# A gather of expert rows through six buffers in place of eight

## The reference, cut to what matters

```python
def peer_ffn(h, wq, sub_keys, u, v):          # 256 tokens, two tiles of 128
    q = (xt @ wq)...                          # 8 heads
    s = einsum(q, sub_keys)                   # 2 x 128 key scores a head
    ...                                       # top 16 of the 16 x 16 sums a head
    expert = i1 * PEER_NKEYS + i2             # 8 heads x 16 = 128 experts a token
    w = jax.nn.softmax(best_s, axis=-1)
    act = jax.nn.gelu(einsum('thkd,td->thk', u[expert], xt))
    return einsum('thk,thkd->td', w * act, v[expert])
```

## Time and profile before

| what | value |
|---|---|
| median of three runs | 1210.49 us (1209.82 to 1211.21) |
| profiled execution, its own time | 1209.58 us |
| its span, first to last instruction | 1207.8 us |
| mean granted TensorE clock | 0.967 |
| PE busy | 1043.4 us, 86% |
| DVE busy | 644.5 us, 53% |
| ACT busy | 378.0 us, 31% |
| POOL busy | 292.5 us, 24% |
| gathers start and end | first issue at 515.66 us, last page taken up at 1177.79 us |

### The profile page before, as it was taken

The page is one execution under the profiler, slowest core; times in us unless marked ns, Lnnn a source line. Parts: engine busy times, 40 slices in busy tenths (PEclk is TensorE's granted clock), DMA queues, the critical chain, the costliest instruction groups (busy, mean ns, idle before and its releaser), DMA issues.

```text
span 1207.8 us, 10043 instructions
## 1 busy us (share of the span) xinstructions
PE 1043.4 (86%) x3443; PEld 581.4 (48%) x3443; DVE 644.5 (53%) x1447; ACT 378.0 (31%) x993; POOL 292.5 (24%) x310
## 2 busy tenths in 40 slices
PE   6999899999999999989996777777789777777777
PEld 5886458444885575765552323222334322222223
DVE  2515436222331265568777888888764545544442
ACT  0133245112222333144333433433432422222222
POOL 3000000020000000045333334443344534434420
PEclk9999999999969779999999999999989999999999
DMA  8435331334333200489999999999989999999990
GB/s 340 147 132 209 139 139 71 139 140 165 142 129 140 104 1 11 198 347 419 423 423 418 421 421 420 422 413 421 421 339 418 419 421 420 421 421 421 420 389 17
DMA packets 43299, 344.88 MB, mean 286 GB/s; under 512 B 4816, under 2 KB 4944, under 8 KB 6000
## 3 DMA queue, kind: packets, MB, share of 16 engines
q0 software_dynamic: 37200, 269.63, 54.1%
q1 hardware_dynamic: 6048, 74.61, 16.5%
HBM read 343.17 MB, written 1.05 MB: 285 GB/s over the span
## 4 chain that ended last, share of the span: by engine, by line
PE 58%; DMA 29%; DVE 7%; ACT 4%; issue 2%; SPq 0%; POOL 0%; POOLq 0%; DVEq 0%; ACTq 0%
PE pp L897 15%; DMA ring<-in_peer_uv,xl 15%; DMA tail<-in_peer_uv,xl 10%; PE pp L474 9%; PE pp L484 5%; PE pp L866 4%; PE pp L934 2%; PE pp L502 2%; PE pp L609 2%; PE pp L587 2%; PE pp L629 2%; DMA sm<-in_peer_uv,xl 2%; PE pa L652 2%; DVE ring L1818 2%; PE pp L794 2%; PE pp L498 2%
## 5 line engine op out<-in xcount | busy, mean ns | idle before, releaser
L897 PE MATMUL pp<-ring,diag 128*128 128x512 f32 x384 | 182.9, 610 | 36.3 <-ACT diag L1247 36.3
L1818 DVE CUSTOM_DVE_ANT_0 ring<-ring,vv 128x1024 f32<-128x1024 f32 x96 | 117.5, 1224 | 74.8 <-DMA ring<-in_peer_uv,xl 74.4
L1233 ACT ACTIVATE small<-small 128x2 f32<-128x2 f32 x128 | 26.1, 204 | 405.5 <-DVE small L1818 405.5
L897 PEld LDWEIGHTS pp<-ring,diag 128*128 128x128 f32 x384 | 72.0, 194 | 132.8 <-issue 74.6
L438 POOL DMA_INDIRECT ring<-in_peer_uv,xl x96 | 96.4, 1004 | 134.5 <-PE pp L897 132.1
L474 PE MATMUL pp<-hT,ring 128*128 128x256 f32 x512 | 114.0, 385 | 3.1 <-DMA ring<-in_wall 3.1
L474 PEld LDWEIGHTS pp<-hT,ring 128*128 128x128 f32 x512 | 98.9, 194 | 17.7 <-issue 3.9
L897 PE MATMUL pp<-ga,diag 128*128 128x512 f32 x128 | 64.3, 626 | 36.7 <-ACT diag L1247 36.7
L897 PE MATMUL pp<-sm,diag 128*128 128x512 f32 x128 | 64.4, 626 | 32.4 <-ACT diag L1247 32.3
L438 POOL DMA_INDIRECT ga<-in_peer_uv,xl x32 | 38.2, 1193 | 222.1 <-issue 142.2
L1247 ACT ACTIVATE diag<-ident,small 128x128 f32<-128x128 f32 x256 | 89.1, 394 | 5.3 <-PE pp L897 1.2
(11 more groups left out here) (363 smaller groups left out, 1574.2 us busy)
## 6 DMA issues: line engine op xcount, KB each, us to landing
ring<-in_wall SPq DMA_DIRECT2D x34, 2048.0 KB, 7.8
ring<-in_peer_uv,xl POOLq DMA_INDIRECT x96, 13.4
xs<-in_x SPq DMA_DIRECT2D x2, 512.0 KB, 3.8
post_g<-in_rows POOLq DMA_DIRECT2D x2, 512.0 KB, 8.4
lt<-in_sub_keys SPq DMA_DIRECT2D x1, 1024.0 KB, 9.9
out<-xs SPq DMA_DIRECT2D x4, 256.0 KB, 4.6
ga<-in_peer_uv,xl POOLq DMA_INDIRECT x32
gl<-in_peer_uv,xl POOLq DMA_INDIRECT x32, 13.0
```

The source lines that it names most:

```text
L897: ins = nc.tensor.matmul(pp[:, t, c, :], diag[:, n * P:(n + 1) * P], rows_uv[g % NBUF][:, D + c * HALF:D + (c + 1) * HALF], start=False, s ...
L1233: nc.scalar.activation(acts[:, at:at + BATCH], dots[:, at:at + BATCH], ACT.Gelu_apprx_tanh)\
L1818: V.tensor_tensor_reduce(out=row_u, in0=row_u, in1=vv[:, t * D:(t + 1) * D], scale=1.0, scalar=0.0, op0=ALU.mult, op1=ALU.add, accum_out=d ...
```

## The change

One constant becomes smaller:

```diff
--- before.py
+++ after.py
@@ -107,7 +107,7 @@
 
 UPDATE_BANKS = (0, 1, 2)
 
-NBUF = 8
+NBUF = 6
 BATCH = 2
 DIAGS = 4
 LAG = 32
```

## The result

Four runs of the changed kernel gave 1234.06 to 1242.49 us, median 1238.7; four of the kernel before gave 1209.82 to 1212.32, median 1210.85. The ratio is 1.0227, with a 95% interval of 1.0182 to 1.0273. The profiled execution took 1234.06 us with a span of 1232.3, against 1209.58 and 1207.8 before. It is the fastest of the four, so the traces are some 3 us less apart than the medians. The prediction was 1215.8 (1212.0 to 1220.5): the sign was right, the size was wrong by a factor of five.

A forecast was written before the change was run, and what follows sets the result against it. The gathers' transfer, 2.49 us a page, was taken as the bound. Steady stretches 0, start 0.3, border 5.0 and end 0 summed to 5.3 us, added to the median 1210.49 for 1215.8 us, range 1212.0 to 1220.5.

The forecast's parts named there:

- What bounds the kernel: Whole gather stage: bound by the transfer itself, 2.49 us a page, with one hole at the border of the tiles.
- The steady stretches, 0 us: Both tiles' steady loops: pages need 5.73 to 6.70 us, six buffers allow 7.62, so no cost.
- The start, 0.3 us: Before the first weight load: page 20 is 0.4 to 1.3 us late, partly absorbed; 0.3 us taken.
- The border, 5.0 us: Between the tiles: after the hole POOL restarts with page 140, not 142, two pages behind; 5.0 us.
- The end, 0: After the last page: nothing is gathered, so the 30 us tail stays as it was; 0 us.
- The first (the border absorbed): Between 887 and 940 us: PE's busy stretch hides the border's delay; 1212.4 us; 0.17 together with the no-change rival.
- The third: Early stretch: up to 1.3 us lost before each of two weight loads, plus border 5.0; 1218.1 us; chance 0.15.
- The fourth (the change does not bind): Whole kernel: an extra buffer might never carry a page, time 1210.5 us; 0.17 together with the absorbed-border rival.
- The second: Steady stretches: loop becomes latency-bound; at 7.9 us a page, 84 pairs lose 23.5 us; 1239.3 us; chance 0.05.
- My marks: Profile signs: steady share stays 1.01, DMA piece falls to about 8.5 us; wrong if dot 158 comes before 936.6.

The follow-up runs named there:

- c_loop: Separate kernel with only the gather loop, seven buffer settings of 40 pages each; six buffers in pairs took 2.490 and 2.481 us a page, eight 2.499 and 2.533.
- p4_second_tile: Kernel before, eight buffers kept; only pages 168 to 255 wait for the sum of page g - 6, the others for g - 8; ratio 1.0063.
- p2_first_tile: Kernel before, eight buffers kept; only pages 48 to 127 wait for the sum of page g - 6, the others for g - 8; ratio 1.0059.
- p1_start: Kernel before, eight buffers kept; only pages 0 to 47 wait for the sum of page g - 6, the others for g - 8; ratio 1.0075.
- p3_border: Kernel before, eight buffers kept; only pages 128 to 167 wait for the sum of page g - 6, the others for g - 8; ratio 1.0087.
- n6_late_norm: Changed kernel (six buffers) with norm_out and the gate portions moved two pages later; ratio 1.0228 to the kernel before.
- e4_pages: Separate kernel that only gathers, 24 pages at each depth from 1 to 8 in flight; a lone page took 5.73 us, four in flight were as good as eight.

## Why the prediction was wrong, by its own steps

**What bounds the kernel** was right: the transfer, at 2.49 us a page. What I missed is that 2.49 us is not a constant of the transfer. It holds while the engines have pages enough.

**The steady stretches, 0 us: the step that failed.** I compared 7.62 us allowed with 5.73 to 6.70 needed, and took a margin that is not used up for a price of zero. In an undisturbed loop that is true, as 14.95 us for six pages shows, and c_loop too. But the kernel is never undisturbed for long, and with 2.9 pages in flight a delay now empties engines. I had also treated the sixteen engines as one: the time from first to last landing report of a page fell from 5.2 to 1.5 us, and the excess of slow packets, most of them at the seams, rose from 4.1 to 20.2 us an engine. Behind the first dot the changed kernel's dots are later than before's by 7.4 us at page 60, 8.6 at 127, 14.1 at 142, 13.0 at 168, 14.1 at 200 and 20.5 at 255. So the steady stretch of the second tile alone cost some 7.5 us, where p4_second_tile measured 0.63%, 7.6 us. The first tile's cost 1 us in this profile, though p2_first_tile measured 0.59% (0.15 to 1.02), 7 us. I can't say why these two differ so much, beyond the 3 us to which one profile is good.

**The start, 0.3 us**, was wrong by the same step: it cost 9.5 us by page 40 and 7.4 by page 60, and p1_start measured 0.75%, 9 us. I had worked out 0.4 to 1.3 us of lateness for page 20 and 22 and priced it as a delay once. PE is full there, so many pages come late, and the rate in this stretch fell to 388 GB/s.

**The border, 5.0 us**, was the right size, and the issue of page 140 in place of 142 behind the hole was the right cause. From page 133 to 142 the dots take 27.2 us (26.9 in p3_border) against 21.8, so 5.4 more. Page 140 goes out at 896.00, when page 142 did before, but for the 10.9 us by which the whole stream was late by then. What I had wrong is the way to 5.0: I took two transfer times of 2.49 us, on the ground that the engines run dry in both kernels. Before, one engine never did, and the pages landed 2.49 us apart across the hole; now none has a packet from 896.03 to 898.60 us. That both ways give 5 us is in part luck. Pages 132 to 135 had also not "long landed": the last report of page 133 comes at 869.40, 0.6 us ahead of its dot. And the wait of DVE that I named as the cause of the hole is not needed for the price, by n6_late_norm. These are the rows of the changed kernel that answer to the earlier trace rows:

```profile
886.46 1.22 DVE L1316 TENSOR_TENSOR hT<-pa,colt 128x1024 f32<-128x1024 f32 x1 [3.27 <-PE pa L926]
...
892.16 3.57 PE L897 MATMUL pp<-sm,diag 128*128 128x512 f32 x4 [4.02 <-ACT diag L1247]
...
896.00 1.91 POOL L438 DMA_INDIRECT sm<-in_peer_uv,xl  x1 [6.25 <-PE pp L897]
898.21 0.98 POOL L438 DMA_INDIRECT tail<-in_peer_uv,xl  x1 [0.30 <-issue]
...
902.86 1.23 DVE L1818 CUSTOM_DVE_ANT_0 sm<-sm,vv 128x1024 f32<-128x1024 f32 x1 [4.47 <-DMA sm<-in_peer_uv,xl]
```

DVE's and PE's waits are the same to the hundredth (3.27 and 4.02), and page 140 took 6.86 us to come in, near the 6.70 of page 142 before.

**The end, 0**, holds for the gathers; 1.5 us came from PE's clock and 2.5 us from a clock fall ahead of the first gather. Both belong to this one execution, and no run ties them to the change.

**The rivals.** The first (the border absorbed) fell: page 158's dot is at 950.51, with 936.6 as its mark. The third named a lateness at the start and priced it at 2.3 us, a quarter of it. The fourth (the change does not bind) fell with the sign. The second had the size by chance: 1239.3 us against 1238.7. It said that every pair is late by a fixed 0.28 us if a page takes 7.9 us where 7.62 are allowed. Undisturbed loops carry on at 14.95 us with a DMA piece of 8.47 us in the chain, so no such fixed loss is there; yet its remarks that late issues eat into the margin and that a short queue lets single slow packets show are what came true. I gave it 0.05, on a margin computed from averages.

**My marks.** "I am wrong if the share falls below 1.0 between 970 and 1170 us" would not have caught it: the share is 1.00. The GB/s beside it fell from 421 to 405. The chain did as forecast (a DMA piece of 8.47 us, 14.95 for six pages), and so could not tell either.

**What stays open.** Which of the kernel's disturbances costs most (the issue with two waits at every 16th page, choosing experts on DVE, PE's full stretches, weight loads) was not separated, nor whether the rows of the experts, which e4_pages and c_loop do not gather, have a part in it. That the engines' drifting apart is what eight buffers buy is read from the traces, and no run sets it by itself. Nor is it explained why a packet is slow behind a pause; e4_pages only shows it.

## What to carry to other kernels

Depth is not the number of buffers but the number of transfers in flight when the next is issued: buffers less those being used. Here some three of eight are always in use, 4.9 in flight cost nothing, 3.9 cost 0.4% and 2.9 cost 2% and more. These prices are of this kernel: its gather loop alone held the full rate with 2.9. A margin worked out from undisturbed latencies tells the rate of an undisturbed loop only. And read the GB/s beside the DMA share: the share can stay full while the rate falls.

## What was not expected of the hardware

- A gather's packets are slower when the engines run dry between pages: a mean of 386 ns with one page in flight, 355 with two, 316 with four. It is the first packets behind the pause (826 ns with one in flight). Idle time and slow packets add up.
- The sixteen parts of a page land 5.2 us apart on the mean with eight buffers and 1.5 us apart with six (pages 48 to 127). The part that comes last sets the pace, and it can work on while the others have run empty, as at a share of 0.07 from 885 to 887 us.
- Six pages by pairs with a consumer hold 422 GB/s alone, and 405 to 411 within the kernel, at a share of 1.00 there.
- A lone page of 1.05 MB takes 5.73 us from issue to use, alone or in the kernel; two in flight are already at 3.00 us a page, filling and draining included.
